# A final normalisation split over the expert steps: one tile beside each step, the rest in a short end stage

## The reference

```python
x = layer_norm(ALPHA * x + fourier_mixer(x, w_in, w_out), ln_g[0], ln_b[0])
# router: sigmoid scores; best of 4 groups of 8 experts, the 2 best experts in that group
y = sum over the token's 2 experts e of gate[e] * (silu(x @ w_gate[e]) * (x @ w_up[e])) @ w_down[e]
x = layer_norm(ALPHA * x + y, ln_g[1], ln_b[1])
```

## Time and profile before

| | |
|---|---|
| median of 3 runs | 2349.26 us (2347.58 to 2349.88) |
| the profiled execution | 2350.37 us, its span 2348.4 us |
| busy | PE 2127.3 (91%), DVE 1373.1 (58%), ACT 998.2 (43%), POOL 582.7 (25%) |
| DMA share of the stretch 0 to 60, 60 to 120, 1000 to 1500 us | 0.60, 0.91, 0.72 |
| first product of the first step | 860.6 us |
| last matmul over; last half of `yrow_b` ready | 2210.3; 2210.7 us |

### The profile page before, as it was taken

The page is one execution under the profiler, slowest core; times in us unless marked ns, Lnnn a source line. Parts: engine busy times, 40 slices in busy tenths (PEclk is TensorE's granted clock), DMA queues, the critical chain, the costliest instruction groups (busy, mean ns, idle before and its releaser), DMA issues.

```text
span 2348.4 us, 37687 instructions
## 1 busy us (share of the span) xinstructions
PE 2127.3 (91%) x12222; PEld 1801.6 (77%) x12223; DVE 1373.1 (58%) x2254; ACT 998.2 (43%) x1442; POOL 582.7 (25%) x493
## 2 busy tenths in 40 slices
PE   8999899999999449999999999999999999999600
PEld 3443678888888349999999999999999999998500
DVE  3321148888887746555655656555555565555298
ACT  1221123333233226555555645655455565554143
POOL 1000034444544411211121121212111121211166
PEclk9999999999999769999999999999999999999855
DMA  6880233443333347767776866877677777766376
GB/s 226 283 287 21 67 126 113 147 147 125 116 127 108 126 153 210 222 203 195 219 216 184 248 194 211 227 223 197 180 220 218 219 218 228 209 202 183 98 286 238
DMA packets 136067, 435.59 MB, mean 185 GB/s; under 512 B 30912, under 2 KB 35008, under 8 KB 131904
## 3 DMA queue, kind: packets, MB, share of 16 engines
q1 hardware_dynamic: 98592, 307.12, 38.6%
q0 software_dynamic: 37440, 128.01, 21.6%
HBM read 328.01 MB, written 108.10 MB: 186 GB/s over the span
## 4 chain that ended last, share of the span: by engine, by line
PE 90%; POOL 3%; issue 3%; DMA 2%; DVE 2%; ACT 0%; SPq 0%; POOLq 0%; ACTq 0%; DVEq 0%
PE ps L877 36%; PE ps L901 15%; PE ps L759 15%; PE ps L696 5%; POOL fin_r L1689 3%; PE ps L865 3%; PE ps L741 3%; PE ps L909 2%; PE ps L715 2%; PE ps L793 2%; PE ps L650 1%; PE ps L780 1%; PE ps L700 1%; PE ps L870 1%; PE ps L659 1%
## 5 line engine op out<-in xcount | busy, mean ns | idle before, releaser
L901 PE MATMUL ps<-wd_hi,hidT 128*128 128x512 f32 x1056 | 293.0, 402 | 0.4 <-ACT hidT L1099 0.4
L1359 DVE TENSOR_TENSOR wd_lo<-wraw,wd_hi 128x1024 fp32r<-128x1024 f32 x132 | 161.9, 1226 | 199.0 <-ACT wd_hi L1057 198.7
L901 PEld LDWEIGHTS ps<-wd_hi,hidT 128*128 128x128 f32 x1056 | 190.1, 189 | 36.3 <-ACT hidT L1099 0.8
L1359 DVE TENSOR_TENSOR wg_lo<-wraw,wg_hi 128x1024 fp32r<-128x1024 f32 x132 | 161.4, 1224 | 92.6 <-ACT wg_hi L1057 92.5
L1632 POOL DMA_INDIRECT sums<-yrow_a,ent_now x33 | 57.2, 1733 | 558.4 <-DVE yrow_a L1422 515.4
L1359 DVE TENSOR_TENSOR wu_lo<-wraw,wu_hi 128x1024 fp32r<-128x1024 f32 x132 | 160.7, 1218 | 52.0 <-ACT wu_hi L1057 51.9
L877 PE MATMUL ps<-mxT_hi,wg_hi 128*128 128x256 f32 (+1 forms) x1056 | 163.3, 297 | 13.4 <-issue 13.4
L1099 ACT CAST hidT<-hid 128x320 fp32r<-128x320 f32 x132 | 60.7, 460 | 257.3 <-DVE hid L1440 257.3
L877 PEld LDWEIGHTS ps<-mxT_hi,wg_hi 128*128 128x128 f32 x1056 | 149.7, 191 | 17.9 <-issue 16.0
L877 PE MATMUL ps<-mxT_lo,wg_hi 128*128 128x256 f32 (+1 forms) x1056 | 163.2, 297 | 0.0
L877 PE MATMUL ps<-mxT_hi,wg_lo 128*128 128x256 f32 (+1 forms) x1056 | 162.6, 297 | 0.0
(11 more groups left out here) (212 smaller groups left out, 4120.0 us busy)
## 6 DMA issues: line engine op xcount, KB each, us to landing
wraw<-expert_w_gate SPq DMA_DIRECT2D x132, 512.0 KB, 5.4
wraw<-expert_w_up SPq DMA_DIRECT2D x132, 512.0 KB, 5.4
wraw<-expert_w_down SPq DMA_DIRECT2D x132, 512.0 KB, 4.4
xch<-x SPq DMA_DIRECT2D x16, 1024.0 KB, 6.7
first_stage<-ych SPq DMA_DIRECT2D x16, 1024.0 KB, 8.3
yt<-first_stage SPq DMA_DIRECT2D x16, 1024.0 KB, 4.9
fin_r<-sums SPq DMA_DIRECT2D x32, 512.0 KB, 3.9
out<-fin_r SPq DMA_DIRECT2D x32, 512.0 KB, 2.9
```

The lines of the kernel that those rows point to most:

```text
L901: mm = nc.tensor.matmul(psY[h], hidT[:, l, c, t * P:(t + 1) * P], wd[r][:, c, cols], start=(i == c == 0), stop=(i == 2 and c == FC - 1))
L1359: nc.vector.tensor_tensor(piece(1, j), wraw[:, j % SLOTS, :], piece(0, j).bitcast(F32), ALU.subtract).then_inc(wlo_ok, 1)
```

## The change

- Besides a list per expert there is a list of tokens per group of experts. Both are whole now, one entry behind the other (`CAP` = 35 x 128 entries each, prefilled: an expert's list with 512 spare rows, a group's with token numbers). In the second stage GpSimd scatters six index columns per block instead of four, the group's two last.
- A second table (`ltab`) is made of the groups' counts. For each step it has the tile of finished tokens to normalise, or a dummy one; a group's tiles are let in from one step behind the group's last. The rest goes to batches of `FB` = 10 tiles, and the table has their number.
- In step u GpSimd scatters the normalised tile (`ln_store`) between the two scatter-adds, which no longer wait for each other, and gathers the rows of the next step's tile behind the gathers for the step after next (`ln_gather`). There is one buffer, `lnrow`.
- VectorE takes the statistics behind the first up quarter, subtracts the mean and multiplies by the gain behind the third, and scales and adds the shift in the down product; ScalarE takes the square root behind the second quarter.
- The end stage gathers ten tiles through GpSimd, does all but the square root on VectorE, and scatters them one after the other.

Cut to its core (the tables and the set-up of the lists are shortened):

```diff
@@ SyncE, expert steps @@
+            sp.wait_ge(ltab_ok, 1)
+            own_wait(sp, glist_out, 32 * GROUPS, sp_gate)
             def load_unit(u, more):
                 e = unit_expert(sp, u)
                 for j in range(PIECES):
                     load_piece(u, e, j)
+                    if j == 5:
+                        tile = ln_slot(u)
+                        own_wait(sp, lent_ok, u, sp_gate)
+                        load_ln_tile(tile)
                     if j == 3 and more:
...
@@ ScalarE @@
+            def ln_deviation(u):
+                act.wait_ge(lvar_ok, u + 1)
+                nc.scalar.activation(lnstd[:, 0:1], lnmv[:, 0, 1:2], ACT.Sqrt, bias=eps2_c).then_inc(lstd_ok, 1)
...
                     act.wait_ge(hid_ok, 4 * u + k + 1)
                     nc.scalar.copy(hidT[:, 0, k, :], hid[:, k % 2, :]).then_inc(hh_ev, 1)
+                    if k == 1:
+                        ln_deviation(u)
...
@@ VectorE @@
+            def ln_statistics(u):
+                dve.wait_ge(lrow_in, 16 * u + 16)
+                step.begin(unit_steps + LN_STEPS * u)
+                statistics(lnrow, 0).then_inc(lvar_ok, 1)
+            def ln_gain(u):
+                dve.wait_ge(lvar_ok, u + 1)
+                nc.vector.scalar_tensor_tensor(lnrow, lnrow, lnmv[:, 0, 0:1], lng2, ALU.subtract, ALU.mult
+                                               ).then_inc(lgain_ok, 1)
+                dve.wait_ge(lstd_ok, u + 1)
+                link(nc.vector.reciprocal(lnrs[:, 0:1], lnstd[:, 0:1]))
+            def ln_shift(u):
+                dve.wait_ge(lgain_ok, u + 1)
+                nc.vector.scalar_tensor_tensor(lnrow, lnrow, lnrs[:, 0:1], lnb2, ALU.mult, ALU.add
+                                               ).then_inc(lfin_ok, 1)
...
                     nc.vector.tensor_tensor(hidT[:, 1, k, :], hid[:, k % 2, :],
                                             hidT[:, 0, k, :].bitcast(F32), ALU.subtract).then_inc(hl_ev, 1)
+                    if k == 0:
+                        ln_statistics(u)
+                    if k == 2:
+                        ln_gain(u)
...
                 nc.vector.tensor_copy(hidC[:, :, LANES:P], hidT[:, 1, :, NARROW:UNIT].bitcast(F32)
                                       ).then_inc(hcl_ev, 1)
+                ln_shift(u)
...
@@ VectorE, end stage @@
+            with dve.Fori(0, batches(dve)) as i:
+                for b in range(FB + 1):
+                    if b < FB:
+                        normal(FB * i + b, i, b)
+                    if b:
+                        gain(FB * i + b - 1, b - 1)
+                        shift(FB * i + b - 1, b - 1)
@@ GpSimd @@
+            def ln_gather(u):
+                own_wait(pool, lent_in, 16 * u + 16, pool_gate)
+                nc.gpsimd.tensor_copy(lent, lent_in_t).then_inc(lent_ok, 1)
+                own_wait(pool, lent_ok, u + 1, pool_gate)
+                pool.indirect_dma_start(lnrow, None, acc, bass.IndirectOffsetOnAxis(ap=lent[:, 0:1], axis=0)
+                                        ).then_inc(lrow_in, 16)
+            def ln_store(u):
+                own_wait(pool, lfin_ok, u + 1, pool_gate)
+                pool.indirect_dma_start(out, bass.IndirectOffsetOnAxis(ap=lent[:, 1:2], axis=0), lnrow, None
+                                        ).then_inc(lrow_out, 16)
             def unit(u, ahead):
                 wide = unit_wide(pool, u)
                 for t in range(2):
                     pool.wait_ge(ya_ok, 2 * u + t + 3)
                     own_wait(pool, yd_ok, 2 * u + t + 3, pool_gate)
-                    if t:
-                        own_wait(pool, y_out, 32 * u + 16, pool_gate)
                     scatter(t, P, y_out)
+                    if t == 0:
+                        ln_store(u)
                 if ahead == 2:
                     turned(u + 1)
                     gather(u + 2)
                     gather_c(u + 2)
-                own_wait(pool, y_out, 32 * u + 32, pool_gate)
+                own_wait(pool, lrow_out, 16 * u + 16, pool_gate)
+                if ahead:
+                    ln_gather(u + 1)
                 with pool.If(wide > 0):
                     own_wait(pool, yc_ok, 2 * u + 4, pool_gate)
                     scatter(2, LANES, yc_out)
                     own_wait(pool, yc_out, 16 * wides_to(pool, u), pool_gate)
+                own_wait(pool, y_out, 32 * u + 32, pool_gate)
...
@@ GpSimd, end stage @@
+            with pool.Fori(0, batches(pool)) as i:
+                own_wait(pool, lents_in, 16 * FB * i + 16 * FB, pool_gate)
                 for b in range(FB):
+                    pool.indirect_dma_start(fin_r[:, b, :], None, acc,
+                                            bass.IndirectOffsetOnAxis(ap=lents[:, b, 0:1], axis=0)
+                                            ).then_inc(fin_in[b], 16)
+                for b in range(FB):
+                    if b:
+                        own_wait(pool, fin_out, 16 * FB * i + 16 * b, pool_gate)
+                    own_wait(pool, fh_ok, FB * i + b + 1, pool_gate)
+                    pool.indirect_dma_start(out, bass.IndirectOffsetOnAxis(ap=lents[:, b, 0:1], axis=0),
+                                            fin_r[:, b, :], None).then_inc(fin_out, 16)
```

More of the change, by code:

```diff
@@ L277, in trunk_kernel @@
         mid = keep.take("mid", CH * NG)
-        padl = keep.take("padl", 2 * USED_ROWS, I32)[0:LANES, :]
+        lent3 = keep.take("lent3", 6, I32)
+        lent_in_t, lent, pad_d = (lent3[:, 2 * i:2 * i + 2] for i in range(3))
+        lents_t = keep.take("lents", 2 * FB, I32)
+        pad_at = keep.byte / 1024
+        padl = [keep.take(n, 2 * CAP // P, I32) for n in ("pad_e", "pad_g")]
+        keep.take("ltab_end", 8)
+        ltab = at("ltab", pad_at, LANES + LN_COLS + 2, I32)[0:1, :]
         def small(name, *dims):
@@ L806, in ranks @@
                 pe.wait_ge(m_ok, g + 1)
-                r0, r1, r2 = (psR[:, i * E:(i + 1) * E] for i in range(3))
+                r0, r1, r2 = (psR[:, i * LISTS:(i + 1) * LISTS] for i in range(3))
                 nc.tensor.matmul(r0, before, msum[:, 0], start=True, stop=True)
@@ L852, in _ @@
             mm.then_inc(utab_ps, 1)
+            pe.wait_ge(lcol_made, 1)
+            for k in range(2):
+                mm = nc.tensor.matmul(psLtab[:, k * P:(k + 1) * P], lcol[:, k:k + 1], ident,
+                                      start=True, stop=True)
+            mm.then_inc(ltab_ps, 1)
             pe.sem_inc(y1_ps, 2)
@@ L1140, in deviation @@
                                      bias=eps2_c).then_inc(fstd_ok, 1)
[L1142 to L1155 removed]
+            with act.Fori(0, batches(act)) as i:
                 for b in range(FB):
[L1157 to L1158 removed]
+                    deviation(FB * i + b, b)
         @block.vector
@@ L1474, in _ @@
             take_xc(0)
+            ln_table()
             dve.sem_inc(yd_ok, 2)
             dve.sem_inc(yc_ok, 2)
+            dve.wait_ge(ln2_in, 32)
+            unit_steps = step.start + step.k
             all_units(dve, unit)
[L1480 to L1485 removed]
+            units = dve.value_load(utab[:, 4 * LANES:4 * LANES + 1], min_val=E, max_val=MAX_UNITS)
@@ L1498, in fin @@
-            def fin(t, i, b):
-                step.begin(start + 2 * t if is_first(t) else start + 2 * t - 1)
-                normal(t, i, b)
-                if not is_first(t):
-                    invert(t - 1, (b - 1) % FB)
-                if not is_first(t, 2):
-                    gain(t - 2, (b - 2) % FB)
-            start = step.start + step.k
-            for b in range(FB):
-                fin(b, 0, b)
-            with dve.Fori(1, TILES // FB) as i:
-                for b in range(FB):
-                    fin(FB * i + b, i, b)
@@ L1513, in _ @@
-            step.begin(start + 2 * TILES - 1)
-            invert(TILES - 1, FB - 1)
-            gain(TILES - 2, FB - 2)
-            gain(TILES - 1, FB - 1)
+                dve.wait_ge(fn_ok, t + 1)
+                nc.vector.scalar_tensor_tensor(fin_r[:, b, :], fin_r[:, b, :], lnmv[:, b % LB, 0:1], lng2,
+                                               ALU.subtract, ALU.mult).then_inc(fg_ok, 1)
+                dve.wait_ge(fstd_ok, t + 1)
+                nc.vector.reciprocal(lnrs[:, b % LB:b % LB + 1], lnstd[:, b % LB:b % LB + 1]).then_inc(fr_ok, 1)
```

291 lines of the change are left out of this document (166 added, 125 removed).

## The result

The changed kernel takes 2401.6 us (median of four runs, 2396.5 to 2408.1), the kernel before 2349.6 on the same chip: ratio 1.0219, 95% interval 1.0188 to 1.0249, so it is **slower by 2.2%**. The prediction was 2358, range 2295 to 2400: the direction was the likelier one, the size was 43 us short. The profiled execution took 2396.5 (span 2394.7, against 2348.4 before).

A forecast was written before the change was run, and what follows sets the result against it. The prediction took TensorE to bound the expert steps, with 129.4 us behind them in which it does nothing. -71.4 + 48.4 + 23.7 + 8 = +8.7 on 2350.4 gave 2359.1 profiled, 2358 for the median; range 2295 to 2400.

The forecast's parts named there:

- The new end: Behind the last matmul: ten leftover tiles gathered, normalised and stored one by one instead of 32 shift additions; 71.4 us less.
- The ring: Up product: VectorE and ScalarE wait on each other, so added passes delay TensorE before the down product; 48.4 us more.
- Lateness of the gather: Narrow steps behind narrow ones: the tile's rows land 2.1 or 2.9 us after statistics want them; 23.7 us more.
- even sharing of the DMA engines: Expert steps: gathers and weight pieces share the DMA engines evenly, so rows land at plus 17.3 and 0.8.
- The clock: Expert steps: TensorE's clock falls after waits, 1.75 us lost each time, in half of nine steps; 8 us more.
- Stages before: Ahead of the expert steps: extra list scatters, tile table and fill rows fit in idle time; 0, at worst 5 us.
- Rival A: Expert steps: the gather lands in time in all steps, only the ring is paid; 2326 us, chance 0.22.
- B: Expert steps: they hide all the added work, VectorE and ScalarE being idle over 40%; 2278 us, chance 0.13.
- C: Expert steps: landing 5 us late, wide steps behind narrow ones wait, clock falls in sixteen steps; 2410 us, chance 0.20.
- D: End stage: over ten tiles are left and a second batch runs, some 50 us more; 2407 us, chance 0.03.
- my case: Whole kernel: the prediction's own forecast, 2358 us, own range 2340 to 2378, chance 0.42.
- the drain: ScalarE's table switches: about 1.38 us more each by the Trainium skill, about 20 us over the steps; left out of the sum.

The follow-up runs named there:

- e8: The changed kernel with the gather of the tile's rows issued ahead of the gathers of the next rows; 2391.9 us, ratio 1.0158 to the kernel before.
- e10: The changed kernel with the wait for the first scatter-add's landing put back between a step's two scatter-adds; 2441.5 us, ratio 1.0367 to the kernel before.

## Why the prediction was wrong

All terms, by the profiled executions, whose spans differ by 46.3 where 8.7 was forecast:

- **The new end: -66.5, forecast -71.4.** Mechanism and number of tiles were right, stores that wait for a landing are even nearer together (4.3, forecast 4.55). The five us are in single places: GpSimd is through with the gathers 22.6 behind the last matmul (forecast 21.6), the first two stores are 6.6 apart, one later pair 6.0, and from the last store's issue to the end it is 6.8, where I had 4.4.
- **The ring: 69, forecast 48.4. This is the step that failed most.** The path was right, piece by piece, and its price was too small. The gain's pass and the reciprocal take 1.54 from the gain's start to hid (1510.76 to 1512.30) where I put 1.19: a reciprocal between two waits isn't 0.05. With 0.04 of roundings that gives 2.85 for a narrow step, forecast 2.46, and 0.94 for a wide one, forecast 0.55, 12.5 us in all. The other 8 are mostly 0.4 to 1.0 more in each wide step ahead of a narrow one, 5.4 in e8: 4.0 of them are idle times of TensorE of 0.3 to 0.9 at the start of the next step (e8's row on "issue", less its one of 9.1 in the first step, which is there before too), whose cause the rows don't name. The rest is in the first and the last step.
- **Lateness of the gather: 24.8, forecast 23.7.** That is what remains of 111.4 behind 69 for the ring and 17.6 for the clock (below), so it takes up their errors. That it fits is in part luck: the rows were forecast for plus 18.1 in three steps and 18.9 in the six with the extra gather, and came at 17.6 and 19.9 in the mean (17.2 to 20.4 in all); the extra gather costs 2.3, not 0.75. Wide steps behind narrow ones were put at nothing and pay about 2.6 in all. That even sharing of the DMA engines is the reason isn't shown by this; that the place in the queue is, e8 shows.
- **The clock: eleven stretches of 1.6, 17.6, forecast 8.** I gave half of nine steps a stretch. It came in eight of them, and in three others (two behind wide ones and the first step) with a single wait of 2.5 too.
- **Stages before: 1.5, forecast 0**, in the run that was predicted. In the later runs of changed kernels 19 to 28 against 860.6, for a bound of 5.

The errors are all of one sign: 20.6 + 1.1 + 9.6 + 4.9 + 1.5 = 37.7, against 37.6 between forecast and measurement. That they close proves nothing, since the lateness is a remainder. The rest of the 43 us of the median is that the profiled execution was the fastest of its four, where I had taken the median to lie 1.1 below it. Rival A (in time) is refuted by the DMA row of 29.4 us, B (all hidden) by the 57.2; C came nearest in its total, 2410, by luck: its lateness of 5 is above the largest found, 4.3, its 11 us for wide steps stand against 2.6 and its 28 for the clock against 17.6, and the ring that it had too small made up for half of that. D didn't happen. The range ended at 2400 between my case and C's 2410, though the unknown sizes all pushed the same way.

Two sums of the prediction don't come out as written: 2217.0 + 1.5 + ten times 1.27 is 2231.2, not 2231.6, and ten tiles at 4.1 behind 2223 end at 2264.0, not 2265.6. And by its own argument that what is put into the ring comes out whole, the drain would cost the sixteen wide steps too, some 44 us and not 20.

The Trainium skill's drain of 1.38 us behind a table switch (ScalarE: Activation LUTs, What ACT_TABLE_LOAD costs) isn't seen after either: load at 1505.63, activation at 1506.93, 1.30. Left out, load and root gave 1.6 back in a narrow step, where load, root and drain would be 2.95.

## What to carry to other kernels

An engine that is idle 40% of the time can still have no room where the work is put: find the stretch in which it does not stand in a ring with the engine that bounds, and put the whole chain (statistics, root, gain, shift) there, even if that is one step later. Where a wait is added for a transfer, put that transfer first in its queue: here that alone gave 28 us back. And a term counted some 30 times should be read off start to start, to a tenth of a microsecond, since here the small omissions all had the same sign.

## What was not expected of the hardware

Half-clock stretches came behind idle pieces of 2.5 us in one step and not in the next of the same kind (e8: narrow steps 6 and 10, the same wait of 2.47, +2.9 and +4.4); each costs about 1.6 us. A wait's idle time in a row can be 0.39 shorter than what it costs, since the matmuls ahead of it are drawn to their modelled ends. The first scatter-add of a narrow step took 9 us to land in e10, that of the last step 6 in the kernel before. And one unchanged program ran its block loop at two paces, 32.5 and 33.6 us per block, in different runs.
